# Sample attention values in a two-layer decoder step: the weighted sum over cached values moved from TensorE to VectorE

## What is computed

```
for i, (win, dil) in enumerate(((128, 1), (512, 4), (2048, 16))):
    idx = lb + arange(t)[:, None] - arange(win // dil + 1)[None, :] * dil
    g = concat([kv_buf, kv_new], axis=1)[:, idx]
    logits = einsum('bthd,btkhd->bthk', q, g[:, :, :, 0]) * SCALE + bias
    o = einsum('bthk,btkhd->bthd', softmax(logits), g[:, :, :, 1])
a = concat([o_i * share_i])          # share_i: the group's part of the denominators
h = x + concat([a, b, c]) @ w_out
```

## Time and profile before

| | |
|---|---|
| median of 3 runs | 1953.53 us (1952.07 to 1956.12) |
| the profiled execution | 1955.55 us, its span 1953.8 us |
| TensorE matmul busy | 1650.4 us, 84% |
| VectorE busy | 1101.7 us, 56% |
| ScalarE, GpSimd busy | 30%, 35% |
| DMA | 729.66 MB moved, mean 373 GB/s |
| TensorE's granted clock | 0.95 of full on the mean |

### The profile page before, as it was taken

How to read it: one execution, slowest core, us unless ns; L and a number is a source line. 1 busy time by engine, 2 the same in 40 slices (tenths; PEclk the granted TensorE clock), 3 DMA queues, 4 the chain that set the end, 5 groups by cost and what they waited for, 6 DMA issues and landing times.

```text
span 1953.8 us, 17246 instructions
## 1 busy us (share of the span) xinstructions
PE 1650.4 (84%) x5336; PEld 862.9 (44%) x5336; DVE 1101.7 (56%) x2718; ACT 587.8 (30%) x1812; POOL 689.4 (35%) x672
## 2 busy tenths in 40 slices
PE   6999999988787878777789999998878878877776
PEld 4777765533333333222247877554333323332221
DVE  2331277877776775444424314878676767645444
ACT  2231133333333332222332301433233323322222
POOL 2130034554444444333211101345444434443431
PEclk8899999989899899999999999999999998899999
DMA  6793879999999999999968747999999999999996
GB/s 194 274 372 141 340 290 421 403 422 421 421 421 421 422 421 422 421 422 422 422 249 327 272 188 281 385 420 402 422 421 421 421 422 421 421 422 421 422 421 287
DMA packets 102484, 729.66 MB, mean 373 GB/s; under 512 B 14827, under 2 KB 15925, under 8 KB 21624
## 3 DMA queue, kind: packets, MB, share of 16 engines
q0 software_dynamic: 90112, 627.43, 77.9%
q1 hardware_dynamic: 11732, 100.48, 13.3%
q10 hardware_dynamic: 548, 0.65, 0.1%
HBM read 724.25 MB, written 48.10 MB: 395 GB/s over the span
## 4 chain that ended last, share of the span: by engine, by line
DMA 43%; PE 43%; DVE 8%; ACT 2%; issue 2%; DVEq 1%; ACTq 1%; POOL 0%; SPq 0%; POOLq 0%
DMA arena<-peer_uv,idx 30%; PE bank L1468 16%; DMA qf<-peer_uv,idx 9%; PE bank L1439 7%; PE bank L1286 6%; PE bank L1281 3%; PE bank L1555 3%; DVE arena L1137 3%; DMA wring<-peer_uv,idx 2%; PE bank L1349 1%; PE bank L1319 1%; DMA yt<-peer_uv,idx 1%; PE bank L1423 1%; ACT diag L735 1%; DVE qf L1137 1%
## 5 line engine op out<-in xcount | busy, mean ns | idle before, releaser
L1468 PE MATMUL bank<-arena,diag 128*128 128x512 f32 (+1 forms) x1456 | 706.3, 630 | 172.6 <-ACT diag L735 172.5
L548 POOL DMA_INDIRECT arena<-peer_uv,idx x364 | 397.9, 1093 | 711.2 <-PE bank L1468 471.7
L1137 DVE SCALAR_TENSOR_TENSOR arena<-arena,xn 128x1024 f32<-128x1024 f32 x364 | 441.2, 1225 | 305.3 <-DMA arena<-peer_uv,idx 303.5
L1468 PEld LDWEIGHTS bank<-arena,diag 128*128 128x128 f32 (+1 forms) x1456 | 269.2, 191 | 580.0 <-issue 316.8
L727 ACT ACTIVATE act<-hid 128x2 f32<-128x2 f32 x288 | 58.6, 203 | 883.1 <-DVE arena L1137 544.4
L1468 PE MATMUL bank<-wring,diag 128*128 128x512 f32 (+1 forms) x352 | 174.1, 634 | 43.0 <-ACT diag L735 43.0
L735 ACT ACTIVATE diag<-ident,weight 128x128 f32<-128x128 f32 (+1 forms) x576 | 194.7, 385 | 20.7 <-issue 1.1
L1468 PE MATMUL bank<-qf,diag 128*128 128x512 f32 (+1 forms) x304 | 149.1, 628 | 38.8 <-ACT diag L735 38.7
L730 ACT ACTIVATE weight<-act,gate 128x1 f32<-128x1 f32 x576 | 138.9, 287 | 20.2 <-issue 0.3
L548 POOL DMA_INDIRECT wring<-peer_uv,idx x88 | 95.2, 1082 | 123.7 <-PE bank L1468 119.0
L1137 DVE SCALAR_TENSOR_TENSOR wring<-wring,xn 128x1024 f32<-128x1024 f32 x88 | 106.7, 1224 | 56.7 <-DMA wring<-peer_uv,idx 56.2
(11 more groups left out here) (261 smaller groups left out, 1465.0 us busy)
## 6 DMA issues: line engine op xcount, KB each, us to landing
kvs<-cache_a_kv_w SPq DMA_DIRECT2D x32, 1022.0 KB, 7.6
wring<-w_col SPq DMA_DIRECT2D x16, 1024.0 KB, 6.1
wring<-w_tok SPq DMA_DIRECT2D x8, 1408.0 KB, 11.6
arena<-peer_wq SPq DMA_DIRECT2D x10, 1024.0 KB, 10.3
wring<-w_out SPq DMA_DIRECT2D x8, 1024.0 KB, 5.0
kvs<-cache_a_kv_w SPq DMA_DIRECT2D x16, 508.0 KB, 7.9
arena<-peer_uv,idx POOLq DMA_INDIRECT x364, 23.6
qf<-cache_keys POOLq DMA_DIRECT2D x10, 576.0 KB, 7.2
```

Source lines behind the costliest of these rows:

```text
L548: pool.indirect_dma_start(out=ring[j], out_offset=None, in_=io["peer_uv"], in_offset=bass.IndirectOffsetOnAxis(ap=idx[:, n:n + 1], axis=0) ...
L1137: last = v.scalar_tensor_tensor(out=ring[j][:, 0:D], in0=ring[j][:, 0:D], scalar=1.0, in1=xn[:, i, :], op0=ALU.mult, op1=ALU.mult, accum_o ...
L1468: last = pe.matmul(bank[b0 + half][0:r, :], diag[:, n % 16, 0:r], ring[SLOT_OF[n]][:, D + 512 * half:D + 512 * half + 512], start=False, s ...
```

## The change

The cached values are no longer multiplied on TensorE. They are loaded transposed, with the 128 dimensions on the partitions and the cache rows along the free dimension (the input array is laid out so beforehand, with the same 576 KB a sequence). The softmaxed probabilities, 64 rows (2 halves x 2 heads x 16 tokens) of 3 x 128, are stored in a DRAM tensor `prows`; for each sequence b they are loaded back so that the 64 partitions of a head all hold the same 4 x 384 probabilities (`load_p`: the source counts 2 rows, each repeated 64 times, of 1536 numbers). VectorE multiplies them with the values in three products and sums over the cache rows (`value_dots`). Two buffers take the probabilities in turn. The new tokens' values stay on TensorE, in a form that gives the transposed result; VectorE adds the two parts.

On VectorE the 8 blocks are spread: 0 before the prompt's first softmax is applied, 1 before T2's product, 2 to 5 after the second, 6 and 7 after the mixer's products, and the convolution now comes after them. On GpSimd the loads of probabilities come before all stores of the layer. `pz`, its memset, the window copies and the transposes go.

```
         pts_ps, pv_ps, pvt_ps                                             (go)
+        pnew_ps = bank[7][:, 0:NG * NS].rearrange("p (g n) -> p g n", g=NG)
+        prows = nc.dram_tensor("prows", (2 * NS, NG * P), F32, kind="Internal").ap()
...
 GpSimd
                 pool.wait_ge(key_ps, NB * l + 1)
                 load_k(l, NB - 1)
-                pool.wait_ge(qk_done, 6 * (l + 1))
-                pool.memset(pz, 0.0).then_inc(pz_clear, 1)
-                for b in range(1, NB - 1):
+                for b in (1, 2, 3, 6):
                     pool.wait_ge(key_ps, NB * l + b + 1)
                     load_v(l, b)
+                pool.wait_ge(qk_done, 6 * (l + 1))
+                load_v(l, 0)
+                load_v(l, 4)
+                pool.wait_ge(prob_done, 3 * l + 1)
+                pool.dma_start(prows.rearrange("r (g n) -> r g n", g=NG), lgs[0:2 * NS, :, 0:P]).then_inc(p_written, 16)
                 pool.wait_ge(key_ps, NB * (l + 1))
-                load_v(l, 0)
-                load_v(l, NB - 1)
+                load_v(l, 5)
+                load_v(l, 7)
+
+                def load_p(b):
+
+                    src = bass.AP(tensor=prows.tensor, offset=(NS * (b // 4) + NT * (b % 4)) * NG * P,
+                                  ap=[[NS // 2 * NG * P, 2], [0, HD], [1, NT * NG * P]])
+                    pool.dma_start(pbs[b % 2], src).then_inc(p_in[b % 2], 16)
+
+                pool.wait_ge(p_written, 16 * (l + 1))
+                load_p(0)
+                load_p(1)
+                for b in range(2, NB):
+                    pool.wait_ge(value_dotted, NB * l + b - 1)
+                    load_p(b)
                 pool.dma_start(io["k_cols"][l], kt[:, :, 0:SEQ]).then_inc(rows_out, 16)
...
 VectorE
+            def value_dots(l, b):
+
+                v.wait_ge(v_in[b], 16 * (l + 1))
+                v.wait_ge(p_in[b % 2], 16 * (4 * l + b // 2 + 1))
...
+                p_ = pbs[b % 2]
+                for g in (1, 2):
+                    v.tensor_tensor(pvq[:, :, g, :], p_[:, :, g, :], vc[b][:, 4 * (g - 1):4 * g, :], ALU.mult)
+                v.tensor_tensor(pvq[:, :, 0, :], p_[:, :, 0, :], vc[b][:, 8, :].unsqueeze(1).broadcast_to([P, NT, P]), ALU.mult).then_inc(value_dotted, 1)
+                v.drain()
+                v.tensor_reduce(yo[:, :, NT * b:NT * b + NT].rearrange("p g t -> p t g"), pvq, AX.X, ALU.add)
+                v.drain()
...
+                value_dots(l, 7)
+                v.wait_ge(pnew_sum, l + 1)
+                v.tensor_tensor(yt[:, 0:3, SEQ:TOKENS], pnew_ps, yo[:, :, :], ALU.add).then_inc(yas_done, 1)
+                conv_taps(l)
+                conv_keep(l)
...
 TensorE
                 pe.wait_ge(probt_done, 3 * l + 2)
-                for g in range(NG):
-                    pe.matmul(pv_ps[:, g, :], ptn[0:NS, g, :], kvn[:, 1, g * P:(g + 1) * P], start=(g == 0), stop=False)
-
-            def sample_values(l, b):
...
+                for h in range(HEADS):
+                    r = slice(64 * (h % 2), 64 * (h % 2) + 64)
+                    p_ = ptn[0:NS, h // 2, :].rearrange("p (a h m) -> p a h m", a=2, h=2)[:, :, h % 2, :]
+                    last = pe.matmul(pnew_ps[r, h // 2, :], kvn[:, 1, h * HD:h * HD + HD], p_, start=True, stop=True)
+                last.then_inc(pnew_sum, 1)
...
                 new_values(l)
-                for b in range(1, 5):
-                    sample_values(l, b)
                 out(l, "u2")
                 turn_probs(l, 2, 0)
-                for b in (5, 6, 0, 7):
-                    sample_values(l, b)
```

More of the change, by code:

```diff
@@ L273, in trunk @@
         ptn = take(NG * 2 * NS).rearrange("p (g n) -> p g n", g=NG)
-        pvs = take(NG * P).rearrange("p (g n) -> p g n", g=NG)
+        yo = take(NG * NS).rearrange("p (g n) -> p g n", g=NG)
         tail = take(9 * P).rearrange("p (c n) -> p c n", c=9)
@@ L278, in trunk @@
         kc += [cand[:, 0:9 * P].rearrange("p (c n) -> p c n", c=9), scores[:, 0:9 * P].rearrange("p (c n) -> p c n", c=9), tail, kc[0]]
-        vc = [flat_xn[:, 0:9 * P].rearrange("p (c n) -> p c n", c=9)] + kc[1:]
+        vc = [arena[:, s * 9 * P:(s + 1) * 9 * P].rearrange("p (c n) -> p c n", c=9) for s in range(3)]
+        vc = [vc[0], kc[1], kc[2], kc[3], vc[1], vc[2], tail, kc[0]]
+        pbs = [t[:, 0:NT * NG * P].rearrange("p (t g n) -> p t g n", t=NT, g=NG) for t in (scores, cand)]
+        pvq = flat_xn[:, 0:NT * NG * P].rearrange("p (t g n) -> p t g n", t=NT, g=NG)
         def near_windows(buf):
@@ L661, in sample_prob_copy @@
                 a.wait_ge(probt_ps, 3 * l + 1)
[L662 to L668, removed]
-                a.activation(ptn[0:NS, :, :], ptn_ps, ACT.Copy).then_inc(probt_done, 1)
[L671 to L683, removed]
+                a.activation(ptn[0:NS, :, :], ptn_ps, ACT.Copy).then_inc(probt_done, 1)
             def prob_copy(l, slot, q):
@@ L1178, in _ @@
                 softmax_max(l, P, lgp[:, 0])
+                value_dots(l, 1)
                 conv_in(l, 2, "T2")
                 softmax_share(l, 2, P, lgp[:, 0])
-                conv_taps(l)
-                conv_keep(l)
+                for b in range(2, 6):
+                    value_dots(l, b)
                 v.wait_ge(in_ps, len(OUTS) * l + OUTS.index("mx1") + 1)
@@ L1338, in new_values @@
                 pe.wait_ge(probt_done, 3 * l + 2)
-                for g in range(NG):
-                    pe.matmul(pv_ps[:, g, :], ptn[0:NS, g, :], kvn[:, 1, g * P:(g + 1) * P], start=(g == 0), stop=False)
-            def sample_values(l, b):
[L1344 to L1351, removed]
-            def turn_sample_values(l):
-                pe.wait_ge(pv_copied, l + 1)
-                pe.wait_ge(probt_done, 3 * l + 3)
-                for g in range(NG):
-                    last = pe.transpose(pvt_ps[:, g, :], pvs[0:2 * NS, g, :], ident[0:2 * NS, 0:2 * NS])
-                last.then_inc(pvt_done, 1)
+                for h in range(HEADS):
[3 more added lines that the diff above has]
+                last.then_inc(pnew_sum, 1)
             def logits(l, q):
@@ L1538, in _ @@
                 mix(l, 2)
-                turn_sample_values(l)
                 out(l, "gb0")
@@ L1662, in laid_out @@
     arrays["cache_keys"] = np.ascontiguousarray(rows[:, :, :, :, 0].transpose(0, 1, 4, 3, 2))
-    arrays["cache_values"] = np.ascontiguousarray(rows[:, :, :, :, 1])
+    arrays["cache_values"] = np.ascontiguousarray(rows[:, :, :, :, 1].transpose(0, 1, 4, 3, 2))
     rows = np.stack([inputs["peer_u"], inputs["peer_v"]], axis=2)
```

18 lines of the change are left out of this document (9 added, 9 removed).

## The result

The changed kernel takes 2094.64 us (median of 4 runs, 2089.41 to 2098.48), the kernel before 1954.82 beside it: a ratio of 1.072, 95% interval 1.070 to 1.074, 139.8 us slower. Forecast were 2077 us and a range of 2015 to 2110. The profiled execution took 2098.48 us with a span of 2096.7, 142.9 more than the span of before. Of the version with halves (experiment 1) one execution of six took 3061 us at a granted clock of 0.57; it is left out of that version's time.

The account below looks back on a forecast made before the run. TensorE's matmul chain was taken to bound both changed stretches; waits for two-engine probability loads add 59.4 us a layer, 61.8 with the clock, 123.6 for two, giving 2079.2, or 2077 against the median; range 2015 to 2110.

Parts of the forecast that it names:

- The disputed price: Each load of probabilities: two source rows outermost mean two engines, 17.5 us from issue to landing, against 5.1 for all engines.
- Step 1: Layer 0: probabilities ready at 119.2 us; GpSimd's write lands and the first two loads are issued at 124.
- Step 2: First loads, sharing engines with SP's bursts: 124 + 17.5 + 6.6 + 5.0 = 153.1 us.
- Steps 3 and 4: VectorE: block 0 ends at 156.9, softmax at 159.6, TensorE's transposes wait 20 us; block 1's products end, load 3 leaves at 164.5.
- Step 5: Odd buffer sets the end: loads 3, 5, 7 with products 56.3 us, SP's three bursts 18.2, to 239.0.
- Step 6: VectorE's block 7 (3.8), addition (0.3), convolution (5.5), gate product (1.1): 249.7 us where it was 190.3, +59.4.
- Step 7: TensorE returns from idling at 1.2 GHz instead of 2.4: 2.4 us lost a layer, making +61.8.
- Costed at nothing: GpSimd's fifteen stores of keys, values and rows behind load 7's wait: time enough to issue them, 9 us of cover left.
- The first rival: All 16 engines carry the loads, landing in 5.1 us, up to 8.1: 1942.5 us, 1940 against the median; chance 13%.
- The second rival: All 16 engines, first load late: each us after 132 costs 1 us a layer; at 138 about 1955 us; chance 3%.

Follow-up runs that it names:

- experiment 1: Changed kernel with each load of probabilities issued as two DMAs of 64 partitions, so 16 engines carry it (the halves): 1961.15 us, ratio 1.005.
- Experiment 4: Changed kernel with 11 of 32 copies of old cache rows a layer, issued by SP while probabilities load, left out: 2066.92 us, ratio 1.058.
- a pattern that can't compute the result: Changed kernel with each load's source one row read 128 times, by all partitions, instead of two rows read 64 times: 1954.37 us, ratio 1.0005.

## Why the prediction was right, and where its sizes were off

The disputed price was taken right: two engines a load, 17.9 us undisturbed for 17.5 forecast, and another pair for the other buffer (share 0.25, loads 0 and 1 landing 28.7 and 29.4 us after issue; in turn they would have needed 15 us more). The Trainium skill's page "DMA: Bandwidth & Descriptors" adds to the rule cited ahead, in the same section, that on GpSimd's path such a transfer takes consecutive engines from a round-robin cursor; the 0.25 agrees. The sum came out 16 us short of 139.8 (19 short in the profiled execution, the longest of the four). Step by step, layer 0, with 0.85 us of the difference being a later start:

- *Step 1, first loads at 124.* They left at 128.08. The write took 7.4 us to land and not 4.8: mis-sized by 3.2 us beyond the later start. The sum named the value loads queued ahead of it and gave them too little.
- *Step 2, landing after 29.1 us.* 28.7. The packets, though, only begin at 132.8, and the last two value loads, ahead in GpSimd's own queue, landed at 129.52 and 135.55; so some of what was put down to SP's bursts is likely theirs. Right size, partly by luck: cause incomplete.
- *Steps 3 and 4.* A block takes 1.29 + 0.68 + 1.75 us and its gaps, 3.8 as forecast; L1383 waits 23.5 us for 20, the late loads; load 3 leaves at 168.40 for 164.5.
- *Step 5, the odd buffer.* 239.0 was forecast, 249.86 measured: 3.9 inherited, 3.9 in load 3 (33.0 for 29.1), 0.9 and 1.5 in loads 5 and 7, and 0.3 twice for the products, after which the load leaves 2.2 us after its block's start and not 1.9. Experiment 4 shows that bursts and loads add, and that the copies were overpriced (14.1 and 10.4 for 17.3), so load 3's excess isn't theirs; without copies it still took 27.3 us against 22.5. Both cases have loads 2 and 3 and two bursts in flight at once. What it is stays open.
- *Step 6.* 10.7 forecast from block 7's start to the end of the gate product, 10.7 measured. Removing the sweep was put at 14.8 a layer: 14.8.
- *Step 7, clock.* TensorE had been idle for 27.96 us, and the first stretch of the projection, 260 to 264, was granted 0.50, that is 1.2 GHz; it cost 1.9 us more in layer 0 and 2.8 in layer 1, 2.4 were taken. (The 0.77 of the prediction is the window from 2.4 us behind the start of L1439 on, not the first 4 us.)
- *Costed at nothing.* The stores of rows behind load 7's wait did no harm; the last two left at 259.85 and 260.58, and the last landed at 262.28.

The first rival, all 16 engines, was forecast at 1942.5 in its own frame and 1940 against the median. Built, it is 1961 with halves and 1954 with a pattern that can't compute the result. Its mechanism was right, its landing times were not: it had the loads at 407 GB/s and 5.1 us, up to 8.1 beside a burst, and halves move 227 and take 6 to 11 us, the first two 13 and 20. The second rival's condition, a late first load, came true with it: block 0 started 20.7 us behind the end of the probabilities (115.40) where the first rival had 12.8, and at 1 us a layer for each us (an estimate by that rival's own rule, not tested by itself) that is 8 of the 11 us a layer by which halves missed 1940. Had the first rival been the forecast, the sign would have been wrong as well.

## What to carry to other kernels

Before costing a DMA by its bytes, look at the outermost count of both sides: for 2, 4 and 8 it was the number of engines here, and a leading count of 2 made a load of some 5 us one of 18, eight times a layer. Splitting such a load so that all 16 engines have a share is a two-line edit and brought back 130 of 140 us. Which partitions are written at one time matters as well: two DMAs of 16 engines, one on each half of the partitions, stayed at 227 GB/s, and DMAs of 8 engines on both halves at once reached 387. Work taken off the busiest engine is worth what it held of the path (14.8 us here) only while whatever feeds its replacement is faster; and the same new order of work gained nothing with the DMA engines full and 11.5 us with time left on them.

## What the runs showed of the hardware that was not expected

- Sixteen engines writing 64 partitions move 227 GB/s, writing 128 partitions 378, from the same kind of source (0.42 us against 0.234 a packet). DMAs of 8 engines on both halves at once move 387. Four and eight engines on 128 partitions were slowed too, to 0.32 and 0.37.
- Reading one DRAM row 128 times costs nothing extra: 0.234 us a packet.
- A two-engine load comes with 896 more packets under 512 B than one on all engines; 64 for each engine without a share would give that number. The page's packet counts tell it.
- Releasing a burst at another time didn't remove the wait for it here, it moved: a load of 28.7 us became one of 45.6 when TensorE ran ahead.
